# Value products of a decode attention spread over a step instead of standing in one group

## The reference

```python
proj = rmsnorm(x, g_mix) @ w_in            # b_a, c_a, h_a, u_b, v_b, q_c, k_c, v_c, f_c
...
# prompt, per block of 128 queries: causal, with a cumulative forget term c
s = q @ k.T * scale + c_q - c_k
p = softmax(where(causal, s, -inf)); o = p @ v
...
# samples: all cached keys and values of 16 pages per sample
s_past = q @ k_past.T * scale + suffix
p = softmax(concat([s_past, s_new]))
o = p[:, :P] @ v_past + p[:, P:] @ v_new
```

## Time and profile before

| | |
|---|---|
| median of 3 runs | 1018.1 us (1015.02 to 1021.15) |
| the profiled execution | 1013.72 us |
| its span, first to last instruction | 1011.9 us |
| mean granted TensorE clock | 0.919 of full speed |
| PE busy | 857.7 us, 85% |
| DVE, ACT, POOL busy | 348.3, 196.2, 262.1 us |
| DMA moved | 316.47 MB |

### The profile page before, as it was taken

One profiled execution on the slowest core, in us unless ns is written; L12 is line 12 of the kernel. 1 busy time (PEld: TensorE's weight loads), 2 busy tenths in 40 slices (PEclk: granted clock), 3 DMA queues, 4 the chain that ended last, 5 costly groups with the idle time before them and its releaser, 6 DMA issues.

```text
span 1011.9 us, 11581 instructions
## 1 busy us (share of the span) xinstructions
PE 857.7 (85%) x4281; PEld 445.9 (44%) x4281; DVE 348.3 (34%) x710; ACT 196.2 (19%) x395; POOL 262.1 (26%) x342
## 2 busy tenths in 40 slices
PE   5999877988999997699999677878788778984994
PEld 3888655655663545344433233333333333331441
DVE  5799967427425566231000000000000000002652
ACT  3110234433232120122111101010110101101431
POOL 6989866222310000211111111010111111001110
PEclk9999978998999997699999889998897989997998
DMA  9899955369976225399999999999999999997111
GB/s 305 320 345 374 328 216 207 142 235 387 371 280 272 84 104 221 120 408 410 416 400 402 411 388 420 402 413 405 419 406 416 391 404 410 427 403 305 58 42 42
DMA packets 53835, 316.47 MB, mean 313 GB/s; under 512 B 11247, under 2 KB 24111, under 8 KB 33049
## 3 DMA queue, kind: packets, MB, share of 16 engines
q1 hardware_dynamic: 34736, 233.28, 57.7%
q0 software_dynamic: 14480, 76.17, 19.8%
q10 hardware_dynamic: 4576, 6.46, 1.8%
HBM read 309.31 MB, written 14.82 MB: 320 GB/s over the span
## 4 chain that ended last, share of the span: by engine, by line
PE 30%; DMA 27%; DVE 1%; issue 1%; SPq 0%; ACT 0%; POOL 0%; POOLq 0%; DVEq 0%; ACTq 0%
DMA arena<-in_w_up 25%; PE psum L1680 16%; PE psum L1797 5%; PE psum L1695 3%; PE psum L1649 1%; DMA arena<-in_w_down 1%; PE psum L1671 1%; DMA moe_rows<-arena,indices 1%; PE psum L488 1%; PE psum L1688 0%; SPq L585 0%; DVE arena L2428 0%; PE psum L1780 0%; PE psum L1526 0%; DMA arena<-h_rows,indices 0%
## 5 line engine op out<-in xcount | busy, mean ns | idle before, releaser
L1680 PE MATMUL psum<-arena 128*64 128x512 f32 x1024 | 261.9, 670 | 67.2 <-DMA arena<-in_w_up 67.2
L1680 PEld LDWEIGHTS psum<-arena 128*64 128x64 f32 x1024 | 87.3, 153 | 217.3 <-issue 216.5
L2394 DVE TENSOR_TENSOR arena<-arena,psum 64x512 f32<-64x512 f32 x32 | 22.1, 692 | 371.2 <-ACT arena L1131 371.2
L1695 PE MATMUL psum<-arena 128*64 128x512 f32 x512 | 115.8, 592 | 1.9 <-DMA arena<-in_w_down 1.9
L1280 PE MATMUL psum<-arena 128*128 128x260 f32 x384 | 86.5, 388 | 0.0
L724 POOL TENSOR_TENSOR arena<-arena 128x2048 f32<-128x2048 f32 x18 | 81.6, 4540 | 0.9 <-DMA arena<-in_cache_k,indices 0.6
L1362 PE MATMUL psum<-arena 128*128 128x260 f32 x320 | 78.5, 398 | 2.5 <-DVEq L1961 2.5
L793 POOL COPY indices<-row_list 128x1 int32 (+1 forms) x26 | 4.6, 178 | 292.9 <-ACT arena L1137 292.9
L1280 PEld LDWEIGHTS psum<-arena 128*128 128x128 f32 x384 | 73.9, 193 | 12.3 <-issue 0.8
L1131 ACT ACTIVATE arena<-psum 64x512 f32<-64x512 f32 x32 | 18.9, 590 | 307.8 <-PE psum L1680 307.8
L1869 DVE TENSOR_REDUCE arena<-arena 128x32 f32<-128x2048 f32 x32 | 72.0, 2280 | 4.6 <-POOL arena L724 3.5
(11 more groups left out here) (331 smaller groups left out, 862.6 us busy)
## 6 DMA issues: line engine op xcount, KB each, us to landing
arena<-in_w_down SPq DMA_DIRECT2D x32, 2048.0 KB, 25.3
arena<-in_w_gate SPq DMA_DIRECT2D x31, 2048.0 KB, 18.5
arena<-in_w_up SPq DMA_DIRECT2D x31, 2048.0 KB, 23.0
arena<-in_w_in SPq DMA_DIRECT2D x11, 1024.0 KB, 9.4
arena<-in_x_prompt SPq DMA_DIRECT2D x8, 512.0 KB, 6.4
arena<-in_w_ple_gate SPq DMA_DIRECT2D x1, 4096.0 KB, 24.6
arena<-moe_rows SPq DMA_DIRECT2D x4, 1024.0 KB, 8.5
out<-arena ACTq DMA_DIRECT2D x8, 256.0 KB, 4.4
```

What stands on the lines that cost most here:

```text
L1680: last = mm(bank(s)[m * SLOTS:(m + 1) * SLOTS, :], hgT[s][:, k, :], w_gu[s][m][:, k, :], start=(k == 0), stop=(k == DC - 1))
L1695: last = mm(bank(6 + s)[n * SLOTS:(n + 1) * SLOTS, :], actT[s][:, k, :], w_dn[s][:, k, n * BANK:(n + 1) * BANK], start=(k == 0), stop=(k = ...
```

## The change

The chunks of a step no longer stand in one group behind the transposes. The first stands right behind query_keys, the second behind the two rest steps, the third behind the transposes, and a fourth, if the step has one, behind the third rest step and spread_gv. The tables, the other engines' programs and all semaphores stay.

```diff
             for s in range(STEPS + 1):
+                chunks = VALUES_AT.get(s, ())
                 if s < STEPS:
                     query_keys(s)
+                for n in chunks[:1]:
+                    values(n)
                 for n in rest_steps[s][:2]:
                     rest_step(n)
+                for n in chunks[1:2]:
+                    values(n)
                 if s == 4:
                     sample_max(True)
                 if s:
                     transpose_p(s - 1)
-                for n in VALUES_AT.get(s, ()):
+                for n in chunks[2:3]:
                     values(n)
                 for h, when in CK_STEP.items():
...
                     rest_step(n)
                 if s in GV_STEP:
                     spread_gv(GV_STEP[s])
+                for n in chunks[3:]:
+                    values(n)
                 if s == 4:
                     sample_max(False)
```

## The result

The changed kernel takes 1025.11 us in the median of ten runs, the kernel before 1018.18 in as many: a ratio of 1.0069 with an interval of 1.0045 to 1.0093. It is 6.9 us slower. The forecast was +3.2 us and "same"; the time lies in the range given, on the other side of 0.5%.

What follows compares the result with a forecast made beforehand. PE's chain of attention, output projection and routing was taken as the bound: 4.2 + 2.3 - 1.3 - 0.8 - 3.7 = +0.7 us, plus 2.5 for the clock, +3.2 on 1018.1, gave 1021.3 us; range 1015 to 1027.

Steps and rivals of the forecast that it cites:

- Steps 6 and 7: PE newly waits 4.2 and 2.3 us for operands DVE spreads; the 1.27 us wait before value chunk 6 goes.
- Steps 9 and 10: DVE still holds the scores of step 11, so only 0.8 us of 4.2 us of waits is won.
- Steps 13 to 15: Waits of value chunks 23, 24, 28 and 31 on their gathers go, winning 3.7 us.
- rival C: Gathers stay late in steps 13 to 15, the 3.7 us is not won: +6.9 us, 1025.0, slower; chance 0.13.
- The clock: PE's granted clock falls once more, behind step 6's new wait: +2.5 us; no fall in step 7.
- Rival B: The clock falls twice, also behind step 7's wait: +5.7 us, 1023.8, slower; chance 0.17.
- A: The forecast itself: 1021 us, own range 1018 to 1023.5, same; chance 0.64.
- The last of the signs: Weighing of values, first output projection and every expert come some 3 us later than in the kernel before.
- The step that failed: On PE no value chunk, spread of c or spread of gating values is added or dropped; only waits cost.

Runs made afterwards that it cites:

- spread_early: The changed kernel with DVE spreading the operands of steps 6 and 7 one step ahead; 0.9945 of the kernel before.
- before_norms: The kernel before, values still grouped, with the layer norms of DVE's step 9 dealt out over steps 9 to 12; one run, 1020.73 us.
- norms_split: spread_early with the layer norms of DVE's step 9 dealt out over steps 9 to 12; 0.9941 of the kernel before.
- group_front: The kernel before with the whole value group right behind the scores from step 9 on; one run, 1023.09 us.
- filler: The changed kernel with eight matmuls whose result nothing reads, in the wait of step 6; one run, 1022.92 us.
- cut_more: norms_split with the second chunk of each step cut in two around the second rest step; one run, 1019.37 us.
- grouped_both: The kernel before, values grouped, with spreads of chunks 0 to 6 one step earlier and layer norms dealt out; one run, 1018.14 us.
- early_only: The kernel before with the new order in steps 6 and 7 alone; 1.0083 of the kernel before.
- two_and_two: norms_split with each step's first two chunks behind the rest steps and the others behind the spreads; 0.9981 of the kernel before.
- late_only: The kernel before with the new order from step 9 on alone; 0.9979 of the kernel before.
- w_o_later: norms_split with the first two parts of w_o waiting for the scores of step 11; 0.9924 of the kernel before.

## Why the prediction was right in its steps and too small in its sum

*Steps 6 and 7.* Forecast 4.2 and 2.3, less 1.3 for V6; measured 4.21, 2.35 and V6's 1.27 gone. That DVE's place for the spreads is the cause is shown by spread_early, which moves nothing else.

*Steps 9 and 10.* Forecast: DVE takes the gain back and leaves 0.8. It does: before_norms shows that grouped the norms cost no more than the 0.34 ahead of Q(11), norms_split that spread they are the whole of that wait, 3.43 in the changed kernel. But Q(9) to Q(11) took 22.20 us for 22.42, so 0.2 was won and not 0.8, since C came ahead of one V and behind three breaks.

*Steps 13 to 15.* Forecast 3.7 won; those waits all went, so rival C did not come about. group_front shows that the spacing does it.

*The clock.* One fall more in step 6, forecast at 2.5, measured at 1.66 there, and 0.36 more than before at Q(11): +2.0. Rival B, a second fall in step 7, did not come in the changed kernel, but a fall at that place did in filler; the two are near enough to each other to count.

*The sum.* The forecast was +3.2; the stretch has 0.7 more of waits (in steps 9 and 10), 0.5 less of clock and 2.9 of cuts. The time lies outside A's own range of 1018 to 1023.5, and the case that came, slower by over 0.5%, had been given 0.30. It lies in the wide range only because that took in B and C, neither of which happened; that it equals C's 1025.0 is chance. The last of the signs failed with the sum: the last W comes 6.5 us later and the first expert 7.9, where 3 was forecast.

*The step that failed* is the sentence "No V, C or G is added or dropped, so the price is only in waits". The matmuls are the same, yet PE's work at full clock is 101.3 us grouped and 104.1 spread. The trace of before had the row: three chunks in a run took 2.73 us from 192.63 to the next start, one alone (205.21) 1.00. So a run costs 0.135 us and a chunk 0.865. Besides, a pair of rest steps takes 3.62 us from its start to the next ahead of transposes (196.78) and 3.71 ahead of a value chunk (206.55 after), and six transposes take 0.74 behind rest steps (200.40) and 0.80 behind a value chunk (211.26 after). PE before:

```profile
195.36 0.44 PE L1347 MATMUL psum<-arena 128*128 128x128 f32 x2
...
196.78 3.77 PE L1362 MATMUL psum<-arena 128*128 128x260 f32 x16
200.40 0.82 PE L1386 MATMUL psum<-arena 128*128 128x128 f32 x6
201.14 2.80 PE L1426 MATMUL psum<-arena 128*32 128x256 f32 x48
...
206.21 0.44 PE L1347 MATMUL psum<-arena 128*128 128x128 f32 x2
```

There are 30 runs for 9; but each of the seven gather waits of before also cut a run, so 14 breaks are new. 14 times 0.135, nine times 0.09 and nine times 0.06 are 3.2 us, for the 2.9 found; about 0.2 us a break, or 0.17 by cut_more (3.1 us for 18). The other kernels lie on the same line. Their work (stretch less waits, less what the slow rows lost) is 101.2 to 101.5 us with 16 or 17 runs (before, group_front, before_norms, grouped_both), 102.3 with 20 (early_only), 102.2 with 21 (two_and_two), 103.5 with 26 (late_only) and 104.1 to 104.4 with 30 or 31 (after, spread_early, norms_split, w_o_later), where a wait inside a group counts as the end of a run. Of the three terms the trace of before showed only the first: 1.9 us, so a forecast of +5.1, right at 0.5%. With all three it would have been +6.4, slower by 0.6%. Why PE loses 0.135 us at the head or tail of a run was not isolated.

## What to carry to other kernels

Before work is moved ahead on an in-order engine, find for each piece the producer that its old place happened to cover; here a table that was right for one order was one step late for the next, and mending the table, not the order, made the change pay. A wait that a neighbour's lateness hides comes out as soon as the neighbour is mended, so walk the chain one wait further: gathers, then DVE, then gathers again. And price a cut itself: from a run of n pieces and a lone piece in the trace work out what a run costs besides its pieces, multiply that by the number of new cuts, and expect the neighbours to lose something too.

## What the runs showed of the hardware

Cutting a run of value matmuls (weights of 128x32, 256 columns) with others between costs PE time here at full clock and without any wait: 0.135 us a run, 0.17 to 0.2 with what it does to the neighbours. A wait of 2.35 us ended without a fall of the granted clock in the changed kernel, and one of 2.34 us at the same place in filler with a fall from 2.4 to 1.2 GHz, worth 1.6 us. V24's wait of 1.38 us was followed by a fall in before_norms, and the same wait of 1.38 us in the kernel before by none. In before_norms V6's wait of 1.60 us was followed by a fall; the wait of 1.64 us for DVE that stands behind step 8's rest step in all thirteen kernels was followed by none in any. So the length of a wait alone does not say whether the clock falls.
